# Recurrence of a gated delta rule: triangular-inverse products on all 64 columns, ScalarE copies and exponentials at other places

## The reference

```python
def step(S, inp):
    rt, wt, kt, vt, kkt, bt = inp
    sk = einsum('bhij,bhj->bhi', S, kkt)
    S = S * wt[:, :, None, :] - sk[..., None] * bt[:, :, None, :] + vt[..., None] * kt[:, :, None, :]
    return S, einsum('bhij,bhj->bhi', S, rt)
S, ys = lax.scan(step, S0, xs, reverse=reverse)
```

## Time and profile before

| | us |
|---|---|
| median of 3 runs | 3180.49 |
| lowest and highest of them | 3178.87, 3200.59 |
| the profiled execution | 3174.54 |
| its span in the profile | 3172.7 |
| the recurrence (stages -1 to 13) in that span | about 590 to 1020 |
| busy in the span: PE, DVE, ACT, POOL | 3061.0, 2173.6, 591.7, 222.5 |
| granted PE clock over the span (share of full) | 0.982 |

### The profile page before, as it was taken

One profiled execution on the slowest core, in us unless ns is written; L12 is line 12 of the kernel. 1 busy time (PEld: TensorE's weight loads), 2 busy tenths in 40 slices (PEclk: granted clock), 3 DMA queues, 4 the chain that ended last, 5 costly groups with the idle time before them and its releaser, 6 DMA issues.

```text
span 3172.7 us, 64856 instructions
## 1 busy us (share of the span) xinstructions
PE 3061.0 (96%) x28080; PEld 2826.2 (89%) x28080; DVE 2173.6 (69%) x4714; ACT 591.7 (19%) x1211; POOL 222.5 (7%) x240
## 2 busy tenths in 40 slices
PE   7999999898899999999999999999999999999999
PEld 4888875577778999999899999999899999999998
DVE  4887967556654576775667566786676676776675
ACT  2000010345443111111111101141110112320111
POOL 1000010122112001000000000010000000000000
PEclk9999999899989999999999999999999999999999
DMA  7556665100000355545254573334345443344343
GB/s 300 186 214 237 262 236 211 37 7 10 8 7 2 120 173 174 172 164 199 77 176 166 197 245 122 132 133 156 131 165 179 171 147 120 133 140 168 127 171 120
DMA packets 68655, 467.52 MB, mean 147 GB/s; under 512 B 7233, under 2 KB 9921, under 8 KB 14106
## 3 DMA queue, kind: packets, MB, share of 16 engines
q1 hardware_dynamic: 51120, 369.12, 33.1%
q0 software_dynamic: 12192, 87.04, 7.4%
q10 hardware_dynamic: 5065, 7.27, 0.8%
HBM read 457.64 MB, written 5.77 MB: 146 GB/s over the span
## 4 chain that ended last, share of the span: by engine, by line
PE 90%; DVE 5%; ACT 3%; DMA 1%; issue 1%; ACTq 0%; DVEq 0%; SPq 0%
PE ps L943 32%; PE ps L1495 18%; PE ps L1014 8%; PE ps L1640 4%; PE ps L1041 4%; PE ps L1079 4%; PE ps L799 2%; PE ps L1139 1%; PE ps L877 1%; PE ps L1118 1%; PE ps L1514 1%; PE ps L1570 1%; PE ps L1544 1%; PE ps L1439 1%; PE ps L1182 1%; PE ps L1132 1%
## 5 line engine op out<-in xcount | busy, mean ns | idle before, releaser
L943 PE MATMUL ps<-arena 128*128 128x128 f32 x4328 | 510.6, 275 | 0.0
L943 PEld LDWEIGHTS ps<-arena 128*128 128x128 f32 x4328 | 496.7, 192 | 0.0
L943 PE MATMUL ps<-arena,ring 128*128 128x128 f32 x2176 | 270.3, 275 | 0.0
L943 PEld LDWEIGHTS ps<-arena,ring 128*128 128x128 f32 x2176 | 256.4, 192 | 0.0
L2187 DVE TENSOR_TENSOR arena<-arena,ps 128x256 f32<-128x256 f32 x143 | 60.2, 421 | 282.5 <-ACT arena L1713 258.3
L1495 PE MATMUL ps<-y,arena 128*128 128x128 f32 x1560 | 191.2, 278 | 5.0 <-DVE arena L2139 5.0
L1495 PEld LDWEIGHTS ps<-y,arena 128*128 128x128 f32 x1560 | 182.6, 194 | 8.8 <-DVE arena L2139 5.2
L2335 DVE CUSTOM_DVE_ANT_0 arena<-arena,vec 128x1024 f32<-128x1024 f32 x152 | 187.3, 1281 | 0.0
L2152 DVE TENSOR_TENSOR arena<-ring 128x512 f32<-128x512 f32 (+1 forms) x167 | 112.3, 672 | 54.5 <-DMA ring<-in_w_f_down 27.0
L1495 PE MATMUL ps<-h,ring 128*128 128x128 f32 x1040 | 128.4, 276 | 0.8 <-ACT h L2073 0.8
L1722 ACT ACTIVATE sg<-arena 128x256 f32<-128x256 f32 x107 | 44.6, 417 | 444.3 <-DVE arena L2196 444.3
(11 more groups left out here) (453 smaller groups left out, 5951.4 us busy)
## 6 DMA issues: line engine op xcount, KB each, us to landing
ring<-in_w_f_gu SPq DMA_DIRECT2D x88, 1024.0 KB, 4.9
arena<-in_ada_t POOLq DMA_DIRECT2D x72, 1024.0 KB, 6.4
ring<-in_w_f_down SPq DMA_DIRECT2D x48, 1024.0 KB, 4.9
ring<-in_w_fx_gu SPq DMA_DIRECT2D x44, 1024.0 KB, 4.8
ring<-in_w_fx_down SPq DMA_DIRECT2D x24, 1024.0 KB, 4.9
ring<-in_w_qk_a SPq DMA_DIRECT2D x18, 1024.0 KB, 5.3
ring<-in_w_qk_r SPq DMA_DIRECT2D x16, 1024.0 KB, 4.8
ring<-in_w_v_r SPq DMA_DIRECT2D x16, 1024.0 KB, 4.9
```

The costliest lines, as they stand in the source:

```text
L943: last = mm(out, weights[number][:, j * P:(j + 1) * P], inputs[number](base + j), start=(s.opens and j == 0 and number in (1, 5)), stop=(s ...
```

## The change

It has five parts.

1. `level_t` on all columns: each product now streams 64 columns (32 before), and its result lies at its own place in PSUM, not packed. Number and order of the products stay. DVE subtracts the same 256 elements a row as before, now read from PSUM in runs with gaps of the same size between.
2. `own_blocks` moves on ACT from level 5 (ahead of place 10) to the end of level 6, behind place 12.
3. `exponents` is cut in two: the small one and `p_inv_f` stay, `ex` and `own` become `exponents_on`, at place 7 of an even unit and place 3 of an odd one. In `scaled` the two products with `p_inv_f` now wait only for the first half.
4. `key_norm` on PE waits for the first pair of sigmoids (`act.sig_first`), which read the bank it writes, and no longer for the second.
5. `first_blocks_t` of an even unit moves on DVE from place 12 to place 11, ahead of `joined` and of the copy of the last chunk's output.

```diff
-                            last = mm(blocks(ps[rows, hd, c * 32:c * 32 + 32], lev), tri_t[held, q, hd, c],
-                                      moved(x_sb[held, hd, c], u, lev, 0), start=True, stop=True)
+                            last = mm(ps[rows, hd, cols(c)], tri_t[held, q, hd, c], x_sb[held, hd, c],
+                                      start=True, stop=True)
...
-                            out = (4 * hd + c) * 32
-                            last = mm(blocks(ps[rows, TWIN, out:out + 32], lev), x_sb[rows, hd, c],
-                                      moved(tri_t[rows, q, hd, c], u, lev, 1), start=True, stop=True)
+                            last = mm(ps[rows, TWIN, at(hd, c)], x_sb[rows, hd, c], tri_t[rows, q, hd, c],
+                                      start=True, stop=True)
...
-                own = tri[rows, q].rearrange("p h c (b two s) -> p h (c b) two s", two=2, s=2 ** lev)[:, :, :, u % 2]
-                tt(own, own, by_head(P)[rows].rearrange("p h (b s) -> p h b s", s=2 ** lev), ALU.subtract) \
-                    .then_inc(*step(f"dve.t{u}_{lev}"))
+                halves = lambda ap: ap.rearrange("p h (b two s) -> p h b two s", two=2, s=2 ** lev)[:, :, :, u % 2]
+                own = halves(tri[rows, q].rearrange("p h c t -> p h (c t)"))
+                tt(own, own, halves(by_head()[rows]), ALU.subtract).then_inc(*step(f"dve.t{u}_{lev}"))
...
-                    pe.wait_ge(*past(f"act.sig{t}"))
+                    pe.wait_ge(*past(f"act.sig_first{t}"))
...
                 f(p_inv_f, own, ACT.Exp, scale=-sign).then_inc(*step(f"act.exp_mid{u}"))
+
+            def exponents_on(u):
+                d = u % 2
+                own, ex, sign = (cum_f, cum2_f, -DS) if d == 0 else (cum2_f, cum_f, DS)
                 act.wait_ge(*past(f"act.exp_mid{u}"))
                 f(ex, ex, ACT.Exp, scale=sign)
                 f(own, own, ACT.Exp, scale=sign).then_inc(*step(f"act.exp{u}"))
...
-                        if unit(p):
-                            own_blocks(p)
                     fill(p, 2 * lev)
+                    if lev == LEVELS and unit(p):
+                        own_blocks(p)
```

More of the change, by code:

```diff
@@ L569, in facing, with by_head @@
             return rows if hd == 0 else (SECOND if rows == FIRST else FIRST)
-        def by_head(n=256):
-            return ps[:, 0:2, 0:n]
+        def by_head():
+            return ps[:, 0:2, 0:256]
         def moved(ap, u, lev, transposed):
@@ L578, in moved @@
             return ap.rearrange("p (b two s) -> p b two s", two=2, s=size)[:, :, (u + transposed) % 2]
-        def blocks(ap, lev):
-            return ap.rearrange("p (b s) -> p b s", s=2 ** lev)
         def readout_of(p):
@@ L1890, in fill @@
                             fourier_out()
+                    elif n == 7:
+                        exponents_on(u)
                     elif n == 9:
@@ L1898, in fill @@
                         key_rate(u)
+                    elif n == 3:
+                        exponents_on(u)
                     elif n == 7:
@@ L2604, in level_done @@
                 rows = sides(u)[0] if lev == LEVELS - 1 else slice(0, P)
-                own = tri[rows, q].rearrange("p h c (b two s) -> p h (c b) two s", two=2, s=2 ** lev)[:, :, :, u % 2]
-                tt(own, own, by_head(P)[rows].rearrange("p h (b s) -> p h b s", s=2 ** lev), ALU.subtract) \
-                    .then_inc(*step(f"dve.t{u}_{lev}"))
+                halves = lambda ap: ap.rearrange("p h (b two s) -> p h b two s", two=2, s=2 ** lev)[:, :, :, u % 2]
+                own = halves(tri[rows, q].rearrange("p h c t -> p h (c t)"))
+                tt(own, own, halves(by_head()[rows]), ALU.subtract).then_inc(*step(f"dve.t{u}_{lev}"))
                 v.wait_ge(*past(f"pe.tt{u}_{lev}"))
                 own = moved(tri_t[:, q].rearrange("p h c t -> p (h c t)"), u, lev, 1)
-                tt(own, own, blocks(ps[:, TWIN, 0:256], lev), ALU.subtract).then_inc(*step(f"dve.tt{u}_{lev}"))
+                tt(own, own, moved(ps[:, TWIN, :], u, lev, 1), ALU.subtract).then_inc(*step(f"dve.tt{u}_{lev}"))
             def first_blocks_t(u):
@@ L2682, in scaled @@
                 own, ex = (cum, cum2) if d == 0 else (cum2, cum)
-                v.wait_ge(*past(f"act.exp{u}"))
+                v.wait_ge(*past(f"act.exp_mid{u}"))
                 v.wait_ge(*past(f"dve.bb{u}"))
@@ L2686, in scaled @@
                 tt(kt_, kd, p_inv_f, ALU.mult).then_inc(*step(f"dve.kt{u}"))
+                v.wait_ge(*past(f"act.exp{u}"))
                 tt(kr[:, g, 0:4], kk.rearrange("p (c t) -> p c t", c=4), ex, ALU.mult)
@@ L2731, in fill @@
                         masked_lat(u)
+                        first_blocks_t(u)
                     elif n == 12:
-                        first_blocks_t(u)
                         first_blocks(u)
```

## The result

| | median us | range | runs | granted clock of the runs |
|---|---|---|---|---|
| before | 3182.85 | 3178.87 to 3200.59 | 4 | 0.982 in the profiled one |
| after | 3144.86 | 3143.76 to 3146.94 | 4 | 0.993 in the profiled one |

The ratio is 0.9876, with an interval from 0.9841 to 0.9912: 1.24% faster. The profiled execution of after took 3146.94 us with a span of 3145.0, so the pair of profiles differs by 27.7 us of span. Cut into stages as before (from one L1305, once L1310, to the next), seven of the eleven stages of after read as follows. The columns are those of the earlier trace rows.

A forecast was written before the change was run, and what follows sets the result against it. The recurrence was taken as a chain passing between engines, no engine full, with low clock in some stages. Products +2.5, waits -9.8 and clock -13.5 sum to -20.8 us: 3159.7 against the median, range 3147 to 3178.

The forecast's parts named there:

- The likeliest case: Recurrence: the waits go and wider products end part of the low clock; -20.8 us, to 3159.7, chance 0.42.
- The direct sum of -7.3 us: Recurrence without clock: 9.8 us of removed waits against 2.5 us added by the wider products.
- Even stages: Stages preparing even units: strict copies 0.80 us earlier, `first_blocks_t` 0.1; 3.6 us over four stages, clean stages 33.4.
- Odd stages: Stages preparing odd units: PE's whole level-2 wait for ACT goes, 5.35 us over six; clean stages 34.0.
- the rival in which the waits only move: PE's and ACT's waits become waits for DVE; 3183 us, or 3169 with the clock mended; chance 0.08.
- Wider products: Level products on 64 columns: 0.07 us a level, three of five levels on the path, 2.5 us in all.
- The bound taken from other lines at clock 0.50: Upper price of wider products: L1279's 68 ns an instruction against L1139's 59, so 0.3 us a level.
- the slower rival: DVE's subtractions pay for reading PSUM with gaps, 0.69 us instead of 0.42; 3189 us, chance 0.05.
- Cover: `own_blocks` (1.69 us) at its new place is hidden in 2.76 us of ACT's idle time between stages.
- the clock's term: Low clock in recurrence stages: falls behind level products go, others stay; 13.5 us, between 0 and 20.1 plus some 4.
- The rival in which all low stretches go: All low clock in the recurrence goes, the first stage's included; -31.4 us, to 3149, chance 0.15.
- A second step: -20.8 us taken off the profiled 3174.54 gave 3153.7; off the median 3180.49, 6 us above, 3159.7.

The follow-up runs named there:

- wide_only: The kernel before with only the level products widened to 64 columns, nothing moved: 3161.24 us, ratio 0.9954.
- own_back: The changed kernel with the four block copies back in level 5 of ACT: 3152.07 us, ratio 0.9921.
- exp_whole: The changed kernel with all four exponentials together again ahead of level 2's x copy: 3151.63 us, ratio 0.992.
- key_later: The changed kernel with DVE's key products of odd units at place 4 instead of 2: 3146.05 us, ratio 0.9908.
- all_const: The changed kernel with packed 32-column products, plus idle products of constants at all places tried until then: 3149.16 us, ratio 0.9918.
- changed_again: The changed kernel itself measured once more, beside twenty runs of before: 3148.62 us, ratio 0.9915.
- moves_only: The changed kernel with packed 32-column products back, so parts 2 to 5 alone: 3158.58 us, ratio 0.9944.
- data_fill: The changed kernel with packed 32-column products, plus idle products of data at PE's waits behind `first_level` and two other places: 3157.57 us, ratio 0.9946.
- late_data: The changed kernel with packed 32-column products, plus three idle products of data at each of places 4 and 9 of odd units: 3159.14 us, ratio 0.9931.
- moves_fill: The changed kernel with packed 32-column products, plus idle products of constants behind `first_level` and two other places: 3158.07 us, ratio 0.9943.

## Why the prediction was wrong in size

**The sign and the parts held.** The likeliest case was the right one in kind: the waits go, and the wider products raise the clock. wide_only shows the second without the first. The direct sum of -7.3 us included 1.57 us of the first stage; for the other ten it was the removed 8.2 less some 2.1 for the products, so -6.1. Measured: -6.8. The sum is closer than its parts, which is partly luck: worked out in the same way, the even stages were to give 3.4 us and gave 4.8, the odd ones 2.7 and gave 2.0. What the first stage's 1.57 us brought can't be told from its clock.

- *Even stages.* Forecast 33.4 us, measured 33.3 to 33.4; a wait of 0.2 left, measured 0.21; the square of the keys no longer waits. own_back puts the block copies' part at 0.8 to 0.9, as worked out. `first_blocks_t` gave nothing there (0.1 forecast), but 0.1 to 0.2 in the odd stages. The fifth even stage, which I gave no gain, got it too, once its clock was up.
- *Odd stages.* Forecast 34.0 us, measured 34.4. The wait for ACT went as said, but "in the odd stages DVE itself waits for `key_rate`, which comes earlier with them" was taken for pure gain. It comes 0.2 us behind the start of POOL's multiply, and the key product grows from 0.69 to 1.63 us. This is the rival in which the waits only move, in the odd stages; exp_whole shows the wait for ACT back and the product short, key_later the product short and the wait for DVE gone. The cut of the exponentials is worth 0.2 to 0.3 us a stage and not 1.01; with the product moved too, the stage goes to 33.5.
- *Wider products.* Forecast 0.2 us a stage, measured 0.1 by wide_only; the second group takes 1.10 us with 64 columns and not 1.15. The bound taken from other lines at clock 0.50 was not needed.
- *DVE's strided source.* 417 ns: the slower rival falls.
- *Cover.* The block copies lie behind 1.17 us of ACT's idle time left, as said.

**The step that failed is the size of the clock's term.** I let those falls go that began behind a level's products and kept those at a stage's start and at the level-2 wait: 13.5 us. In the profiled pair the clock gave 20.1 us in five stages and up to 3.4 in the first, 23.5 at most: the falls of the second kind went too. The split by what stands just ahead of a fall was mistaken. Widening alone and moving alone each took the low time over 580 to 1020 us from 78.5 to 27.3 us, both together to 6.8, and all_const had 17.1; filler at some places only left the runs at 0.987, even where a fall had stood. The rival in which all low stretches go came nearest, with its 3149 (changed_again gave 3148.6, the first measurement 3144.86), at a chance of 0.15 where the forecast had 0.42.

**A second step was weak.** I took the change off the profiled execution and then off the median 6 us above it, as if the two differed by something that stays. Of the 38.0 us between the medians, 27.6 are those of the profiled pair. The other 10.4 are where the two profiled executions lie among their runs: 8.3 below the median before, 2.1 above it after. Over the 79 runs of before in the five groups the granted clock goes from 0.973 (3205.05 us) to 0.987 (3165.19), and the time falls by 28.9 us for 0.010 of clock, in a nearly straight line. So the runs of before differ in the main by their low clock, and a change that takes away low clock takes that with it; this fits the runs of after lying within 3.2 us and those of before within 21.7. For the 6 us themselves it is shown in part: on the line the profiled execution's 0.982 stands for 3177.7.

The same line, drawn on beyond its data to 0.993, gives 3145.9, which is the profiled run's time of after but for 1 us. That agreement is luck. It leaves nothing for the direct effect of 6.8 us, and its 31.8 us from 0.982 to 0.993 are more than the 23.5 at most that the stages show.

**Between the rules on the clock.** wide_only keeps the waits, adds columns and goes from 0.983, the median beside it, to 0.990; so idle gaps alone don't set the level. moves_only takes some 7 us out of the stages' waits and goes to 0.987, with the columns as they were; so the waits count as well. Of the Trainium skill's two statements ("TensorE: Matmul & The Clock Gate", What's actually happening, and HAM oscillation) the first, that activity releases the throttle, fits both; the rule on gaps covers at most the second, and a forecast by it alone would have missed the 15.5 us of wide_only.

**Open.** How exactly the level follows the work is not settled: either group widened gives more than half of the gain, idle products in some places none, and in all places as much as both groups. Operands make no difference that was measured (data_fill and late_data against moves_fill and late_const). All of this fits that the added work counts because the array is busier, but that is argued and not shown; no run shows the measure by which the chip goes.

## What to carry over

A kernel that is a chain of narrow products can pay for its thin use of the array in clock, all along the stretch in which it is such a chain (here 440 us; outside it the clock did not change). Count the low stretches of several executions, as they come at different places in each, and allow that a change brings all of them back, not only those beside its place. Products that cost the same with twice the columns are then better wide, and a change that adds columns where PE is the one that works needs a measurement of its own. Where an instruction is made to start earlier, look at what runs on the engines beside it at its new time; a wait removed on one engine came back as a product of over twice the length on another.

## What was not expected of the hardware

- A DVE product of 128 x 512 with both inputs in SBUF took 1.63 us when it began inside a multiply of POOL of 1.31 us, and 0.69 when it began behind it.
- 16 products on quadrants of 64 x 64 (32 instructions) take 0.67 us with 32 columns and 0.69 with 64, on two quadrants 1.10 both times: at full clock the columns were nearly free.
- The granted clock of the kernel before went from 0.973 to 0.987 between executions of one program, and with twice the columns in 3648 instructions of its small products to 0.990, at waits as they were.
- Idle products in waits lengthened no clean stage (34.3 and 33.3 us in all_const, with 3.8 us more of PE work in the odd one), and yet the 96 of moves_fill (192 instructions, 30.2 us of PE) gained nothing while other waits had none.
